# Filler matmuls of identity by ones at the opening and at both layer norms of a decoder layer

## The chip, the cores and the metric

The kernel runs on one core of a Trainium2 chip. A core has a matrix engine (TensorE, PE in the profile), VectorE (DVE), ScalarE (ACT), GpSimd (POOL) and a queue engine that starts transfers (SyncE, SP). TensorE's clock is granted at one of two levels, 1.2 or 2.4 GHz; the profile gives the granted clock of a stretch as a share of the full one. The metric is the device time of one execution in microseconds (us), the median of several runs.

## The reference

One layer of a hybrid decoder is computed for 512 prompt tokens with 16 learned tokens ahead of them, and for 8 single sample tokens. All arithmetic is float32. Cut to what matters here:

```python
x = layer_norm(jnp.concatenate([meta, x_prompt], axis=1), ln_in_g, ln_in_b)
q, k, v, qi, wi, ki, hq, kf, hi, log_f, hg = project(x, w_in[l], lb_all[l])   # x @ w_in, split
# indexer scores -> top-k keys -> attention over them (attn_o)
# gated linear recurrence in chunks of 128 (hg_o), per-head norm and gate
mix = merge_heads(attn_o, hg_o, hg, hg_norm_g[l], w_out[l])                   # ... @ w_out
x = layer_norm(ALPHA * x + mix, ln1_g[l], ln1_b[l])
x = layer_norm(ALPHA * x + swiglu(x, w_gate[l], w_up[l], w_down[l]), ln2_g[l], ln2_b[l])

def layer_norm(x, g, b):
    mu = jnp.mean(xf, -1, keepdims=True)
    var = jnp.mean(jnp.square(xf - mu), -1, keepdims=True)
    return (xf - mu) * lax.rsqrt(var + LN_EPS) * g + b
```

The width is 2048, the inner width of the SwiGLU 5632. The samples take the same path, with keys and values from a paged cache. Outputs are the new x of both kinds of tokens, and the keys, values, indexer keys and states.

## The kernel before, in words

The kernel is written engine by engine: each engine has one block with its instructions in the order in which they run, and semaphores are the only thing that ties them together. So the order of TensorE is that of the text of its block, `def _(pe)`.

The activations lie turned, with the feature index on the 128 partitions and the 536 tokens (16 learned, 8 samples, 512 prompt) in the free dimension; 16 blocks k of 128 features make the width (`KD` = 16). Products run in three passes: ScalarE rounds an operand to a high part, VectorE subtracts it from the operand for the low part, and TensorE adds high by high, high by low and low by high (`wh`, `wl` for weights, `xh`, `xl` for x). The semaphore `h_split` counts ScalarE's parts, `l_split` VectorE's. Weights arrive by transfers that SyncE issues.

Opening. x arrives by tokens and is normalised in place (`xtok`). TensorE turns it block by block: `x_turn(k)` (L1419 and on) makes five transposes, four of 128 tokens and one of the 24 others. ScalarE or VectorE then applies gain and bias (`x_lin0`, `x_lin1`), ScalarE makes `xh`, VectorE `xl` (semaphore `xl_ready`). TensorE does `x_turn(0)`, `x_turn(1)`, and then `two_products`, which waits for the splits of the first two weight tiles (VectorE L1887) and goes through k: in each step `x_step(k)` turns block k + 2 and waits for `xl` of block k, and twelve products of 260 columns follow (L1405).

First layer norm. When the last of the 16 output blocks of the mixer is added (VectorE L2346, semaphore `s_done`), VectorE adds it to a running sum (`finish`, L2321, semaphore `s_sum`) and, after ScalarE has squared it (L1192), to a running sum of squares (L2327, semaphore `q_sum`). Each counts 16 for a layer norm. `ln_sums(1)` on TensorE waits for both at 16 and multiplies a matrix of ones by the sums, which adds over the partitions (L1776 to L1779, results in the PSUM banks b4 to b7). VectorE forms means and variances (L2359 to L2364), ScalarE the reciprocal root, and then each block k is centred (L2372), scaled (L2380), given gain and bias (ScalarE L1253) and split (ScalarE L1256, VectorE L2398). TensorE waits for the split of block 0 and runs `first_pair`: twelve products for the gate weights with each block k, and in every second step twelve more for the up weights (helper `passes`, L1787).

SwiGLU. Gate and up products go by a scheme with seven products of half blocks for eight, whose sums of tokens and weights VectorE forms; hidden values go to memory and come back for the down product, 64 units of 11 blocks each.

Second layer norm. The same, with `ln_sums(2)`. Then TensorE turns the outputs back, in four quarters of 20 transposes (L1367): each quarter waits for four more blocks from ScalarE (L1349, semaphore `y_ready`). ScalarE and VectorE take turns in copying the turned banks out (L1355, L2592), and SyncE writes them.

`mm` is the plain matmul (output, stationary operand, moving operand), `ident` a 128x128 identity and `ones` a 128x128 matrix of ones, both float32. `acc` is four PSUM banks, indexed [:, tile parity, half, column].

Of the kernel before, what the change touches and what calls it, by code (L numbers as in the profile page):

```python
# [14 lines left out]
P = 128  # L15
# [167 lines left out]
def program(  # L183
# [6 lines left out]
    def sem(name):  # L190
        if name not in sems:
            sems[name] = ctx.enter_context(nc.semaphore(name))
        return sems[name]
# [41 lines left out]
    ident = rt.take("ident", [P, P])  # L235
    ones = rt.take("ones", [P, P])
# [163 lines left out]
    acc = ctx.enter_context(nc.psum_tensor("acc", [P, 2, 2, 512], F32))  # L400
# [3 lines left out]
    b7 = ctx.enter_context(nc.psum_tensor("b7", [P, 512], F32))  # L404
# [46 lines left out]
    def y_copied(u):  # L451

        return "y_act" if y_on_act(u) else "y_dve", len([v for v in range(u + 1) if y_on_act(v) == y_on_act(u)])

    def y_bank(u):
        u %= 8
        return (b4, b5, b6, b7)[u][:, :] if u < 4 else acc[:, (u - 4) // 2, u % 2, :]
# [902 lines left out]
    def _(pe):  # L1360
        mm = nc.tensor.matmul

        def turn(out, in_):

            k = in_.shape[0]
            b = in_.start_partition()
            return nc.tensor.transpose(out, in_, ident[b:b + k, b:b + k])  # L1367
# [21 lines left out]

        X = (xh, xl)  # L1390

        def two_products(s, t, before):

            pe.wait_ge(sem("l_split"), (s + 2).v)
            if t.const >= 2:
                for i in range(2):
                    pe.wait_ge(sem(f"acc_read{(t + i).odd}"), (t + i).half().v)
            for k in range(KD):
                before(k)
                for i in range(2):  # L1400
                    s_, t_ = s + i, t + i
                    a_h, a_l = (w[:, s_.odd, k * P:k * P + P] for w in (wh, wl))
                    for n, (a, b) in enumerate(((a_h, X[0]), (a_h, X[1]), (a_l, X[0]))):
                        for half in range(2):
                            ins = mm(acc[:, t_.odd, half, 0:LIVE], a, b[:, k, S0 + half * LIVE:S0 + half * LIVE + LIVE],  # L1405
                                     start=(k == 0 and n == 0), stop=(k == KD - 1 and n == 2))
                    if k == KD - 1:
                        ins.then_inc(sem("mm"), 1)
# [11 lines left out]
        def x_turn(k):  # L1420
            if k == 0:
                pe.wait_ge(sem("x_norm"), NB + 3)
            if k == 1:
                pe.wait_ge(sem("krow_ready"), 1)
            if k >= 2:
                pe.wait_ge(sem(f"x_lin{k % 2}"), k // 2)
            for c in range(NB):
                turn(real[k % 2][:, c * P:c * P + P], xtok[:, c, k * P:k * P + P])
            turn(small[k % 2][:, 0:R0], xtok_s[:, k * P:k * P + P]).then_inc(sem("x_turned"), 1)

        x_turn(0)
        x_turn(1)

        def x_step(k):
            if k + 2 < KD:
                x_turn(k + 2)
            pe.wait_ge(sem("xl_ready"), k + 1)

        def kx_turn(b):
# [5 lines left out]
            last.then_inc(sem("kx_turned"), 1)  # L1445

        two_products(At(0), At(0), x_step)
        for i in (2, 3):
            product(At(i), At(i), KD, P, 0, X, {5 * q + 3: (lambda b=3 * i - 6 + q: kx_turn(b),) for q in range(3)})
# [211 lines left out]
        for g in range(NG):  # L1661
            for j in range(4):
# [7 lines left out]
                else:  # L1670
                    n = 4 * (g - 1) + j
# [96 lines left out]

        def ln_sums(n):

            pe.wait_ge(sem("s_sum"), 16 * n)
            pe.wait_ge(sem("q_sum"), 16 * n)
            if n == 1:
                pe.wait_ge(sem("so_out"), NS)
            ssum = SUMS[n - 1]
            mm(b4[:, :], ones[:], ssum[:, 0, R0:NT], start=True, stop=True)  # L1776
            mm(b5[:, 0:NS], ones[:], ssum[:, 0, S0:R0], start=True, stop=True)
            mm(b6[:, :], ones[:], ssum[:, 1, R0:NT], start=True, stop=True)
            mm(b7[:, 0:NS], ones[:], ssum[:, 1, S0:R0], start=True, stop=True).then_inc(sem("ln_sums"), 1)  # L1779

        ln_sums(1)


        def passes(out, hi_, lo_, x_, xl_, first, last):
# [57 lines left out]
        for u in range(NU):  # L1842
# [8 lines left out]
            for k in range(CK):  # L1851
# [3 lines left out]
                for h in range(2):  # L1855
                    x_, xl_ = (b[c % 2][:, k, h * LIVE:h * LIVE + LIVE] for b in (hh, hl))
                    ins = passes(acc[:, u % 2, h, 0:LIVE], a_h, a_l, x_, xl_, k == 0, k == CK - 1)
            ins.then_inc(sem("mm"), 1)
        ln_sums(2)

        for q in range(4):
            pe.wait_ge(sem("y_ready"), 4 * q + 4)
# [2 lines left out]
            for c in range(NB + 1):  # L1865
                u = 5 * q + c
                if u >= 8:
                    name, n = y_copied(u - 8)
                    pe.wait_ge(sem(name), n)
                for k in range(4):  # L1870
                    out = y_bank(u)[:, P * k:P * k + P]
# [752 lines left out]
```

## Time and profile before

| | |
|---|---|
| median of three runs | 2597.6 us (2593.74 to 2597.88) |
| profiled execution, its own time | 2595.63 us |
| its span, first to last instruction | 2594.1 us |
| TensorE busy | 2513.6 us, 97% |
| VectorE busy | 1579.8 us, 61% |
| ScalarE busy | 967.1 us, 37% |
| mean granted TensorE clock | 0.986 |

The profile is of one execution. Its times count from the first instruction. Matmuls are pipelined, so a matmul's own duration is longer than the distance between the starts of two that follow each other; that distance is what a further one costs. A float32 matmul of full precision leaves two records, one of the three-pass kind leaves one. Some matmul records can be missing. The view of busy times by stretches has for each engine the busy time and in brackets the number of instructions; after POOL stand the granted TensorE clock, the share of the transfer engines and GB/s.

### The profile page before, as it was taken

The numbers are of one execution on the slowest core, as the hardware profiler recorded it, in microseconds if no ns is written. First come the engines' busy times: TensorE is split into PE (matmuls) and PEld (weight loads), VectorE is DVE, ScalarE is ACT, GpSimd is POOL, SyncE is SP. The second block draws the span as 40 slices with busy tenths as digits, with TensorE's granted clock in tenths as the row PEclk, the third lists the DMA queues.
The fourth block names the chain that finished last, engine by engine and source line by source line (L and its number), as shares of the span: only waits on it lengthen the run. The fifth ranks groups of instructions, "written<-read, shape, count | busy, mean of one in ns | idle before, by whom it ended". The sixth has DMA issues, their size and how long they took to land.

```text
span 2594.1 us, 47371 instructions
## 1 busy us (share of the span) xinstructions
PE 2513.6 (97%) x20365; PEld 2452.7 (95%) x20365; DVE 1579.8 (61%) x2225; ACT 967.1 (37%) x1542; POOL 173.1 (7%) x196
## 2 busy tenths in 40 slices
PE   6999999999999999989999999999999999999995
PEld 5989999999999988989999999999999999999995
DVE  6157776776766632588777777777777533333345
ACT  5344434343333422254444444444444321222123
POOL 1111111111000112000000000000000000000003
PEclk9989999999999999989999999999999999999998
DMA  4413333333322433333333333343333643333221
GB/s 137 113 51 83 98 82 82 92 93 87 103 83 77 128 108 93 116 113 107 128 109 128 118 106 131 107 131 115 110 127 109 229 156 103 123 102 110 90 68 66
DMA packets 292172, 279.52 MB, mean 108 GB/s; under 512 B 8344, under 2 KB 266696, under 8 KB 291464
## 3 DMA queue, kind: packets, MB, share of 16 engines
q1 hardware_dynamic: 284656, 255.18, 31.4%
q0 software_dynamic: 7344, 21.80, 2.9%
q8 instruction: 138, 2.26, 0.4%
q14 instruction: 34, 0.28, 0.0%
HBM read 247.54 MB, written 29.42 MB: 107 GB/s over the span
## 4 chain that ended last, share of the span: by engine, by line
PE 93%; DVE 4%; ACT 2%; issue 1%; DMA 1%; SPq 0%; ACTq 0%; DVEq 0%
PE acc L1787 47%; PE acc L1383 30%; PE b L1787 5%; PE b L1367 2%; PE acc L1405 1%; PE b L1528 1%; PE b L1649 1%; PE b L1624 1%; PE b L1544 1%; PE b L1705 1%; PE b L1725 1%; PE b L1556 1%; DVE lnd L2393 1%; PE b L1650 0%; PE b L1506 0%
## 5 line engine op out<-in xcount | busy, mean ns | idle before, releaser
L1383 PE MATMUL acc<-xh,wh 128*128 128x260 f32 (+2 forms) x2144 | 455.8, 294 | 6.1 <-DVE wl L1887 3.7
L1383 PE MATMUL acc<-xl,wh 128*128 128x260 f32 (+2 forms) x2144 | 439.0, 286 | 0.0
L1383 PE MATMUL acc<-xh,wl 128*128 128x260 f32 (+2 forms) x2144 | 438.9, 286 | 0.0
L1242 ACT ACTIVATE ph<-pair 128x1024 fp32r<-128x1024 f32 x252 | 267.3, 1061 | 413.6 <-PE acc L1787 405.2
L2404 DVE TENSOR_TENSOR pl<-pair,ph 128x1024 fp32r<-128x1024 f32 x252 | 308.5, 1224 | 158.9 <-ACT ph L1242 158.9
L1787 PE MATMUL acc<-hh,dh 128*128 128x260 f32 x1408 | 398.3, 283 | 3.6 <-DVE hl L2538 3.6
L1787 PE MATMUL acc<-hl,dh 128*128 128x260 f32 x1408 | 398.0, 283 | 0.0
L1787 PE MATMUL acc<-hh,dl 128*128 128x260 f32 x1408 | 397.8, 283 | 0.0
L1383 PEld LDWEIGHTS acc<-xh,wh 128*128 128x128 f32 (+1 forms) x2144 | 334.9, 191 | 15.2 <-DVE wl L1887 3.9
L1383 PEld LDWEIGHTS acc<-xh,wl 128*128 128x128 f32 (+1 forms) x2144 | 336.0, 191 | 0.0
L1383 PEld LDWEIGHTS acc<-xl,wh 128*128 128x128 f32 (+1 forms) x2144 | 335.8, 191 | 0.0
L1787 PE MATMUL acc<-xh,ph 128*128 128x260 f32 x1008 | 285.9, 284 | 1.4 <-DVE pl L2404 1.4
L1787 PE MATMUL acc<-xl,ph 128*128 128x260 f32 x1008 | 285.6, 283 | 0.0
L1787 PE MATMUL acc<-xt,pl 128*128 128x260 f32 x1008 | 285.3, 283 | 0.0
L1787 PE MATMUL acc<-xh,pl 128*128 128x260 f32 x1008 | 285.1, 283 | 0.0
L1787 PE MATMUL acc<-xtl,ph 128*128 128x260 f32 x1008 | 285.0, 283 | 0.0
L1787 PE MATMUL acc<-xt,ph 128*128 128x260 f32 x1008 | 284.0, 282 | 1.1 <-ACT part L1288 0.6
L1887 DVE TENSOR_TENSOR wl<-raw,wh 128x2048 fp32r<-128x2048 f32 (+1 forms) x69 | 159.0, 2306 | 184.7 <-ACT wh L817 166.7
L1787 PEld LDWEIGHTS acc<-hh,dh 128*128 128x128 f32 x1408 | 265.5, 189 | 4.6 <-DVE hl L2538 4.6
L1787 PEld LDWEIGHTS acc<-hl,dh 128*128 128x128 f32 x1408 | 265.2, 188 | 0.0
L1787 PEld LDWEIGHTS acc<-hh,dl 128*128 128x128 f32 x1408 | 265.1, 188 | 0.0
L817 ACT ACTIVATE wh<-raw 128x2048 fp32r<-128x2048 f32 x68 | 129.6, 1907 | 172.4 <-PE acc L1383 169.8
(436 smaller groups left out, 4441.1 us busy)
## 6 DMA issues: line engine op xcount, KB each, us to landing
raw<-in_w_in_dram SPq DMA_DIRECT2D x52, 1024.0 KB, 5.6
draw<-in_w_down_dram SPq DMA_DIRECT2D x32, 1408.0 KB, 6.6
pair<-in_w_gate_dram SPq DMA_DIRECT2D x42, 1024.0 KB, 5.3
pair<-in_w_up_dram SPq DMA_DIRECT2D x42, 1024.0 KB, 5.0
raw<-in_w_out_dram SPq DMA_DIRECT2D x16, 1024.0 KB, 5.6
hid_dram<-hid SPq DMA_DIRECT2D x22, 520.0 KB, 3.2
stg<-hid_dram SPq DMA_DIRECT2D x44, 260.0 KB, 6.7
sacc<-x_dram SPq DMA_DIRECT2D x6, 1040.0 KB, 7.7
```

The source lines that it names most:

```text
L817: act.activation(wh[:, s.odd, :], raw[:, s.odd, :], ACT.Copy).then_inc(sem("h_split"), 1)
L1242: act.activation(ph[n % 3][:, :, :], block_of(q, i), ACT.Copy).then_inc(sem("h_split"), 1)
L1367: return nc.tensor.transpose(out, in_, ident[b:b + k, b:b + k])
L1383: ins = mm(acc[0:rows, t.odd, half, 0:n_], a, b[:, kx0 + k, lo + half * n_:lo + half * n_ + n_], start=(k == 0 and n == 0), stop=(k == kt ...
L1405: ins = mm(acc[:, t_.odd, half, 0:LIVE], a, b[:, k, S0 + half * LIVE:S0 + half * LIVE + LIVE], start=(k == 0 and n == 0), stop=(k == KD - ...
L1528: last = mm(b7[0:w, P * c + SUB * i:P * c + SUB * i + SUB], et[:, off + c * w:off + c * w + w], qd[:, R0 + P * c + SUB * i:R0 + P * c + SU ...
L1544: last = mm((b6, b7)[b // 4][:, P * (b % 4):P * (b % 4) + P], ident[0:NS, b:b + 1].to_broadcast([NS, P]), itok[0:NS, 5, :], start=True, st ...
L1556: last = mm(b5[:, S0 + b:S0 + b + 1], ss[:, b, :], hq[:, S0 + b:S0 + b + 1], start=True, stop=True)
L1624: mm((b4, b5)[hd][:, 0:w], q[:, hd, lo:lo + P], k[:, R0:R0 + w], start=True, stop=True)
L1787: ins = mm(out, a, b, start=first and n == 0, stop=last and n == 2, skip_group_check=True)
L1887: V.tensor_tensor(wl[:, s.odd, 0:n], raw[:, s.odd, 0:n], fr(wh[:, s.odd, 0:n]), ALU.subtract)\
L2404: V.tensor_tensor(pl[n % 3][:, :, :], block_of(q, i), fr(ph[n % 3][:, :, :]), ALU.subtract).then_inc(sem("l_split"), 1)
```

## The change

A helper `keep_awake(out, count)` on TensorE multiplies the identity by the ones `count` times, into 128 columns of a bank that is free at that time. Nobody reads the result and no semaphore is raised. It is called at five places:

- opening: 20 after `x_turn(1)`, ahead of `two_products`
- in `ln_sums`, thus at both layer norms: 10, ahead of the wait for the last sums, behind a new wait for the last but one of them
- after `ln_sums(1)`: 32; after `ln_sums(2)`: 56

```diff
+        def keep_awake(out, count):
+
+            for _ in range(count):
+                mm(out, ident[:], ones[:], start=True, stop=True)
+
...
         x_turn(0)
         x_turn(1)
+        keep_awake(acc[:, 1, 1, 0:P], 20)
 
...
         def ln_sums(n):
 
+            pe.wait_ge(sem("s_sum"), 16 * n - 1)
+            keep_awake(b7[:, 0:P], 10)
             pe.wait_ge(sem("s_sum"), 16 * n)
             pe.wait_ge(sem("q_sum"), 16 * n)
...
         ln_sums(1)
+        keep_awake(acc[:, 0, 1, 0:P], 32)
 
...
         ln_sums(2)
+        keep_awake(acc[:, 0, 1, 0:P], 56)
```

TensorE at the opening, before. A row is a line, an operation, output<-inputs (moving operand first), the size and how many in a row:

```order
L1367 MATMUL b<-ident,vrows 128x113
L1417 MATMUL b<-ptT,pageof 128x8
L1367 MATMUL b<-ident,xtok 128x128 x4
L1367 MATMUL b<-ident,xtok_s 128x24
L1367 MATMUL b<-ident,xtok 128x128 x4
L1367 MATMUL b<-ident,xtok_s 128x24
L1367 MATMUL b<-ident,xtok 128x128 x4
```

The same place in the changed kernel:

```order
L1367 MATMUL b<-ident,xtok 128x128 x4
L1367 MATMUL b<-ident,xtok_s 128x24
L1395 MATMUL acc<-ones,ident 128x128 x20
L1367 MATMUL b<-ident,xtok 128x128 x4
L1367 MATMUL b<-ident,xtok_s 128x24
L1410 MATMUL acc<-xh,wh 128x260 x2
L1410 MATMUL acc<-xl,wh 128x260 x2
```

Twenty matmuls stand between the turns of block 1 and of block 2; nothing else has moved, only the line numbers.

TensorE at the first layer norm, before (the last products of the mixer, the sums, the first pair):

```order
L1383 MATMUL acc<-xh,wl 128x260 x2
L1776 MATMUL b<-ssum_146,ones 128x512
L1777 MATMUL b<-ssum_146,ones 128x8
L1778 MATMUL b<-ssum_146,ones 128x512
L1779 MATMUL b<-ssum_146,ones 128x8
L1787 MATMUL acc<-xh,fh_153 128x260
```

And in the changed kernel:

```order
L1383 MATMUL acc<-xh,wl 128x260 x2
L1395 MATMUL b<-ones,ident 128x128 x10
L1784 MATMUL b<-ssum_146,ones 128x512
L1785 MATMUL b<-ssum_146,ones 128x8
L1786 MATMUL b<-ssum_146,ones 128x512
L1787 MATMUL b<-ssum_146,ones 128x8
L1395 MATMUL acc<-ones,ident 128x128 x32
L1796 MATMUL acc<-xh,fh_153 128x260
```

Ten stand ahead of the sums and 32 behind them.

TensorE at the second layer norm in the changed kernel (before, the two rows of L1395 are missing):

```order
L1796 MATMUL acc<-hh_186,dl_184 128x260
L1395 MATMUL b<-ones,ident 128x128 x10
L1784 MATMUL b<-ssum_193,ones 128x512
L1785 MATMUL b<-ssum_193,ones 128x8
L1786 MATMUL b<-ssum_193,ones 128x512
L1787 MATMUL b<-ssum_193,ones 128x8
L1395 MATMUL acc<-ones,ident 128x128 x56
L1367 MATMUL b<-ident,sacc 128x128 x16
```

Ten stand ahead of the sums and 56 between them and the turns of the first quarter.

## Rows read from the trace of the kernel before

**Rows 1.** The page: busy time; clock in 40 slices; chain by engine.
```profile
PE 2513.6 (97%) x20365; PEld 2452.7 (95%) x20365; DVE 1579.8 (61%) x2225; ACT 967.1 (37%) x1542; POOL 173.1 (7%) x196
...
PEclk9989999999999999989999999999999999999998
...
PE 93%; DVE 4%; ACT 2%; issue 1%; DMA 1%; SPq 0%; ACTq 0%; DVEq 0%
```

**Rows 2.** Order in time, TensorE, opening: start, us, line, operation, [idle before <-releaser].
```profile
22.46 1.12 PE L1367 MATMUL b<-ident,xtok 128*128 128x128 f32 x4
...
29.32 1.11 PE L1367 MATMUL b<-ident,xtok 128*128 128x128 f32 x4 [4.25 <-DVE wl L1887]
...
33.36 0.96 PE L1367 MATMUL b<-ident,xtok 128*128 128x128 f32 x4
...
35.97 0.60 PE L1367 MATMUL b<-ident,xtok 128*128 128x128 f32 x4
...
38.19 0.60 PE L1367 MATMUL b<-ident,xtok 128*128 128x128 f32 x4
```

**Rows 3.** Order in time, VectorE, opening.
```profile
24.78 4.48 DVE L1887 TENSOR_TENSOR wl<-raw,wh 128x2048 fp32r<-128x2048 f32 x2
29.18 1.34 DVE L1936 TENSOR_TENSOR xl<-lnt,xh 128x536 fp32r<-128x536 f32 x2
...
32.44 0.72 DVE L1936 TENSOR_TENSOR xl<-lnt,xh 128x536 fp32r<-128x536 f32 x1 [0.72 <-ACT xh L864]
```

**Rows 4.** Order in time, TensorE, first layer norm.
```profile
1131.85 1.10 PE L1776 MATMUL b<-ssum,ones 128*128 128x512 f32 x2 [2.36 <-DVE ssum L2321]
...
1134.52 0.44 PE L1779 MATMUL b<-ssum,ones 128*128 128x8 f32 x2
1141.83 0.56 PE L1787 MATMUL acc<-xh,fh 128*128 128x260 f32 x1 [6.87 <-DVE xl L2398]
```

**Rows 5.** Busy time by stretches: stretch, length, engines, clock, transfers.
```profile
1132.90:1135.00 2.10, 2.06 (x7) 0.97 (x5) 2.10 (x2) 0.00 (x0) 0.00 (x0) 0.57 0.00 0
...
1141.80:1146.70 4.90, 4.87 (x22) 4.90 (x23) 4.90 (x9) 3.56 (x6) 0.00 (x0) 0.50 0.17 56
...
2559.50:2569.00 9.50, 0.00 (x0) 0.00 (x0) 8.32 (x7) 4.24 (x7) 8.13 (x6) 0.52 0.00 0
2569.00:2573.30 4.30, 4.20 (x20) 3.79 (x20) 4.27 (x4) 3.26 (x6) 3.46 (x3) 0.50 0.01 4
2573.30:2576.00 2.70, 1.94 (x17) 1.61 (x16) 2.70 (x6) 1.97 (x3) 1.35 (x1) 0.94 0.07 27
```

**Rows 6.** Order in time, all engines, second layer norm.
```profile
2554.57 1.10 PE L1776 MATMUL b<-ssum,ones 128*128 128x512 f32 x2 [2.40 <-DVE ssum L2327]
...
2556.59 0.28 PE L1779 MATMUL b<-ssum,ones 128*128 128x8 f32 x2
...
2568.23 2.96 ACT L1349 ACTIVATE sacc<-lnd,vec 128x520 f32<-128x520 f32 x4 [2.57 <-DVE lnd L2393]
...
2569.10 3.68 PE L1367 MATMUL b<-ident,sacc 128*128 128x128 f32 x16 [12.23 <-ACT sacc L1349]
```

**Rows 7.** Order in time, TensorE, a head's output, all between at 128 columns.
```profile
224.09 0.38 PE L1552 MATMUL b<-aT,itok 128*128 128x128 f32 x2
...
225.87 1.28 PE L1556 MATMUL b<-hq,ss 128*128 128x1 f32 x11
```

**Rows 8.** Order in time, VectorE, first layer norm.
```profile
1132.73 2.29 DVE L2333 TENSOR_TENSOR fl<-first,fh 128x2048 fp32r<-128x2048 f32 x1 [0.98 <-ACT fh L1200]
...
1135.00 0.76 DVE L2359 TENSOR_SCALAR mu<-b 128x512 f32<-128x512 f32 x2
...
1140.98 0.70 DVE L2398 TENSOR_TENSOR xl<-sacc,xh 128x520 fp32r<-128x520 f32 x1 [0.34 <-ACT xh L1256]
...
1142.82 0.69 DVE L2398 TENSOR_TENSOR xl<-sacc,xh 128x520 fp32r<-128x520 f32 x1
```

**Rows 9.** The chain that ended last, in order of time, one piece of SwiGLU.
```profile
1216.01 17.30 PE acc L1787 x144
```

## The prediction

> **What bounds the kernel now.** I read the page's busy line, its clock line and the shares of the chain first [rows 1]. The reader is to see three things: TensorE is busy for 97% of the span, the chain that ends last is 93% TensorE, and the clock granted to TensorE is full nearly everywhere. So the kernel is a stream of matmuls, and only two kinds of time are left to an edit of this sort: places where TensorE stands still, and places where it works at the lower of its two clocks, 1.2 instead of 2.4 GHz. An added matmul in a pause doesn't shorten the pause. It can only raise the clock for what follows. So I went to the three pauses that the edit fills, with the order in time of TensorE and VectorE there, and then to the table by stretches for the granted clock.
>
> Opening: the ten transposes of x, begun at 22.46, end at 25.07, TensorE then stands until 29.32, where VectorE's two splits of the first weights end (24.78 + 4.48), and goes on with steps of one turn and twelve products [rows 2, 3]. The first of these steps takes 33.36 - 29.32 = 4.04 us, the second 2.61, the third 2.22, and so do the following ones. Same instructions, 1.82 times the time: TensorE is at 1.2 GHz until about 34. (The page's clock line shows a 9 for the first slice; it begins with the first recorded change, so here I go by the durations.) First layer norm: pause of 2.36 us before the sums, then, after them, 6.87 us until the first split of x1 is there [rows 4]. The clock falls during the sums (0.57), and is at 0.50 for the first 4.9 us of work after the pause [rows 5]. Second layer norm: 2.40 us before the sums, 12.23 after them, and clock 0.50 in the 4.3 us in which the first turns run [rows 5, 6].
>
> **The price of one added matmul.** It is a 128x128 float32 matrix times 128 float32 columns, two records each. The nearest rows are the eight of that shape and type in a head's output: 224.09 to 225.87 us, so 1.78 / 8 = 0.222 us at full clock [rows 7]. At 1.2 GHz I take twice that, 0.44 (the opening's steps say 1.82 times, 0.40). The added wait (one short of the last sum) never binds: that sum is done while TensorE still multiplies, and nobody waits for the new matmuls, which signal nothing. What they can cost is only to run past the end of the pause.
>
> **Opening, 20 matmuls.** At full clock they take 4.44 us and would end at 29.52; each microsecond of the block that is spent at 1.2 GHz adds half a microsecond. So all hangs on when the clock rises. Rises in the trace came 4.4 to 4.8 us after work resumed at 29.32 (the surplus of the two slow steps is 1.82 + 0.39 = 2.21 us, twice that is 4.4), 4.9 after 1141.83, and some 4.3 after 2569.10 [rows 2, 4 to 6]. In the changed kernel work without a pause begins with the transposes at 22.46, so I expect the rise near 22.46 + 4.6 = 27.1. That is 2.0 us into the block, which then ends at 29.52 + 1.0 = 30.5, or 1.2 us later than TensorE could have gone on. Against that stand the 2.21 us of surplus, since the steps now run at 2.22 from the first. Do the others keep up? The second split of x is ready at 29.18 + 1.34 = 30.52, before the second step at 32.7; the third ends at 32.44 + 0.72 = 33.16 today and is wanted at about 35.5 [rows 3]. Yes. Sum: **-1.0 us**. Bounds: -2.0 if the clock is up from the block's first matmul, +0.3 if it rises only 4.9 us after 25.07 (then the end is 32.0, 2.7 late, against 2.2 to 2.4), +4.6 if it never rises.
>
> Here a rule of the Trainium skill speaks against the change. The row: in the last layer norm nothing but transposes runs from 2569.10, and the clock goes from 0.50 to 0.94 in the stretch after 2573.30 [rows 5, 6]. The page "TensorE: Matmul & The Clock Gate", Part 4 on the PE-mode transpose, says that the full clock isn't engaged by transposes, as they don't count as busy in the same way. By that rule the opening would come out at +0.3, by the row at -1.0; the trace disagrees with the page, and I go by the row.
>
> **First layer norm, 10 and 32 matmuls.** The ten take 2.2 us of the 2.36 that TensorE waits anyway: nothing. They keep the clock up through the sums, whose four products then take 2556.59 - 2554.57 = 2.02 us from first to last instead of 2.67 [rows 4, 6]. But that buys nothing: VectorE works at its own split of a weight until 1135.02 and takes the means at 1135.00 as it is [rows 8]. From there the next thing to come is the same, at 1141.83. The 32 start at about 1134.0 and take 7.1 us, to 1141.1: 0.7 us to spare. Then the first pairs start warm: 4.9 us at 1.2 GHz become 4.9 / 1.82 = 2.7, which saves 2.2. What is late next is x1's second split, ready at 1142.82 + 0.69 = 1143.51 [rows 8], when twelve products of 17.30 / 144 = 0.12 us [rows 9] end at 1143.27: 0.3 us given back. After that a pair of steps costs TensorE 36 x 0.12 = 4.3 us and VectorE 3.7 (its splits start 1.84 us apart, at 1140.98 and 1142.82), so it isn't caught again. The next waits on the way, VectorE's sums of token blocks and the loads of weights, start when TensorE has finished, so they move with it. Sum: **-1.9 us**. Bounds: -2.5 (a before with a longer slow stretch), -1.2 (0.26 us a matmul, so that the 32 run over by 0.7).
>
> **Second layer norm, 10 and 56 matmuls.** The ten are hidden as before. The 56 take 12.4 us from 2556.7, to 2569.1, which is where the fourth output is ready (the first of ScalarE's four pieces from 2568.23) and the turns start at 2569.10 today [rows 6]. The twenty turns then run at full clock, 2.2 us instead of 4.3. But what follows is paced by VectorE, busy for 4.27 of 4.30 us there [rows 5], and its chain of centring and scaling doesn't wait for these turns. So **0 us**, from -0.5 (a copy that ScalarE does earlier) to +1.9: the last twenty turns lie on the path, TensorE pauses three more times before them, and if their rise of the clock comes later than today they take twice as long.
>
> Together -1.0 - 1.9 + 0 = **-2.9 us**. The profiled execution took 2595.63, so it would take 2592.7. The median of the runs shown is 2597.6, 2.0 above it; I set the change against the median: **2594.7 us**, or 0.11% less.
>
> **Rivals.** *The transposes don't count.* Then the opening gives +0.3 to +0.5 and the total is -1.5: 2596.1. For it: in the opening the transposes at 22.46 are followed by a pause, so that place shows nothing; against it the last layer norm.
>
> *The clock's own moments.* The clock falls and rises at moments that the program doesn't set, so a slow stretch in the pauses that stay (before the turns of the last quarters, or between the selection's products) may drop out or be shortened too. With the best bounds, -2.0 - 2.5 - 0.5 = -5.0, and a little from those: 2592.3.
>
> *Slower: identity by ones doesn't hold the clock.* Its operands are constants, mostly zeros, and no row shows a matmul of two constants. If it counts for nothing the clock falls at 1132.9 and 2559.5 as today, and the blocks overrun at 0.44 us each. Opening: 20 x 0.44 = 8.8, end at 33.9, +4.6. First norm: 32 x 0.44 = 14.1 from 1134.7 to 1148.8, +7.0. Second: 12 at full clock, 44 x 0.44 = 19.4, to 2578.9, 9.8 late, of which some 8 reach the end. Total +20: 2617. The point from which it decides is whether the granted clock in the 32 is 1.0: above 0.22 us a matmul the 32 have 0.7 us of room, so from about 0.245 on they cost.
>
> **How the numbers follow.** A measurement here tells about 0.2% (5.2 us) from no change. Forecast, -2.9: 0.66. Transposes don't count: 0.14. More than the sum, about -5: 0.13. Identity by ones doesn't hold the clock: 0.07. Faster by over 0.2% needs more than 5.2 us, which takes the third case and half of it is still short, with a little from the first's tail and from the scatter of the medians: 0.12. Slower is the last case: 0.07. Within 0.2%: 0.81. The runs shown lie 4 us apart, so I add 1.5 us to the cases' ends: from 2592.3 - 1.5 = 2590.8 to 2596.1 + 1.9 (last turns slow) + 0.6 = 2598.6.
>
> **What would show it right or wrong.** Right: in the opening the added line runs from 25.1 to about 30.5, its first five or so matmuls at 0.44 and the rest at 0.222 us, and the third step starts near 35.0 instead of 35.97. In the first norm the granted clock stays at 1.0, the means are still taken behind VectorE's split, the first pair starts no later than before, counted from the end of the product ahead of it, and its 24 first products take 0.12 us each with one short wait. In the second the first turns start within 0.2 us of today's time and the end moves only as far as the start did. Wrong: a granted clock of 0.50 inside the added blocks, a block that ends behind what it waits for, VectorE waiting for turns at the end, or a gain at the first norm that later waits of VectorE take back.

## The result, and the profile after

The changed kernel takes 2590.77 us, median of 20 runs (2586.13 to 2596.93), against 2596.30 of the kernel before in the same measurement (20 runs, 2593.14 to 2599.84): ratio 0.9977, interval 0.9970 to 0.9983. That is 5.5 us less (by the interval 4.4 to 7.8), and 0.03 us below the foot of the stated range. The forecast was 2.9 us less, which lies outside the interval. The direction was right, the size half of what came. Of the 3.9 us between the forecast time of 2594.7 and 2590.77, 1.3 are the start: the forecast counted from the median of three executions, 2597.6, and twenty give 2596.30. A ratio with its interval compares executions taken side by side, so it isn't quite the quotient of the two medians. Two executions of later measurements lie far outside the others (4116 us at a granted clock of 0.56, and 13,894 us) and are left out of every median.

The page of the changed kernel, the lines that answer to [rows 1]: TensorE's busy time, its clock in 40 slices, the chain by engine.

```profile
PE 2535.9 (98%) x20621; PEld 2475.5 (96%) x20621; DVE 1580.1 (61%) x2225; ACT 966.8 (37%) x1542; POOL 173.3 (7%) x196
...
PEclk9999999999999999999999999999999999999999
...
PE 93%; DVE 3%; ACT 2%; issue 1%; DMA 1%; SPq 0%; ACTq 0%; DVEq 0%
```

TensorE is busy 22 us longer, with 256 more records (two for each of the 128 added matmuls), and the kernel is shorter. The three 8s in the clock line of before (a slice is a fortieth of the span) are gone. The profiled execution took 2590.7 us (span 2589.2), 4.9 less than that of before.

The opening in order of time, TensorE (start, us, line, operation), against [rows 2]:

```profile
22.87 1.11 PE L1367 MATMUL b<-ident,xtok 128*128 128x128 f32 x4
...
24.15 5.96 PE L1395 MATMUL acc<-ones,ident 128*128 128x128 f32 x40
29.95 0.60 PE L1367 MATMUL b<-ident,xtok 128*128 128x128 f32 x4
...
32.19 0.60 PE L1367 MATMUL b<-ident,xtok 128*128 128x128 f32 x4
...
34.43 0.60 PE L1367 MATMUL b<-ident,xtok 128*128 128x128 f32 x4
```

The block starts right behind the turns and lasts 29.95 - 24.15 = 5.80 us where 20 x 0.222 = 4.44 were counted at full clock: 1.36 more, so 2.7 us of it were at the lower clock (the record of the granted clock has the rise at 26.76, 2.6 us into the block). From there the steps take 2.24 us from the first. This execution's loads were in 0.9 us sooner, so all times stand that much earlier; measured from the transposes' end (24.15 and 25.07), the third step starts 10.28 us behind it and 10.90 before.

The first layer norm, TensorE, against [rows 4]; the figure in brackets is the pause and what ended it:

```profile
1125.42 2.39 PE L1395 MATMUL b<-ones,ident 128*128 128x128 f32 x20
1127.94 1.10 PE L1784 MATMUL b<-ssum,ones 128*128 128x512 f32 x2
...
1129.95 0.28 PE L1787 MATMUL b<-ssum,ones 128*128 128x8 f32 x2
1130.09 7.39 PE L1395 MATMUL acc<-ones,ident 128*128 128x128 f32 x64
1137.86 0.36 PE L1796 MATMUL acc<-xh,fh 128*128 128x260 f32 x1 [0.38 <-DVE xl L2408]
```

And its granted clock by stretches (TensorE busy, weight loads, VectorE, ScalarE, GpSimd, clock, transfers), against [rows 5]:

```profile
1128.00:1130.00 2.00, 2.00 (x8) 1.04 (x8) 1.19 (x1) 0.78 (x1) 0.00 (x0) 1.00 0.00 0
1130.00:1137.50 7.50, 7.48 (x67) 7.29 (x65) 6.87 (x12) 3.25 (x5) 0.00 (x0) 1.00 0.72 239
1137.80:1141.00 3.20, 3.08 (x23) 2.90 (x24) 3.20 (x6) 2.23 (x4) 0.00 (x0) 1.00 0.20 66
```

The clock stays at 1.0 through the sums, the block and the first pairs. The block of 32 ends 0.38 us before the first split of x1 is there. VectorE, against [rows 8], still works at its split of a weight when the sums are done at 1130.1, and takes the means behind it:

```profile
1128.81 2.29 DVE L2343 TENSOR_TENSOR fl<-first,fh 128x2048 fp32r<-128x2048 f32 x1 [0.98 <-ACT fh L1200]
1131.02 0.76 DVE L2369 TENSOR_SCALAR mu<-b 128x512 f32<-128x512 f32 x2
```

The second layer norm, TensorE, against [rows 6]:

```profile
2546.99 2.39 PE L1395 MATMUL b<-ones,ident 128*128 128x128 f32 x20
2549.56 1.10 PE L1784 MATMUL b<-ssum,ones 128*128 128x512 f32 x2 [0.17 <-DVE ssum L2337]
...
2551.71 12.75 PE L1395 MATMUL acc<-ones,ident 128*128 128x128 f32 x112
2564.30 1.91 PE L1367 MATMUL b<-ident,sacc 128*128 128x128 f32 x16
2566.05 0.60 PE L1367 MATMUL acc<-ident,sacc 128*8 128x128 f32 x4
2569.45 2.63 PE L1367 MATMUL acc<-ident,sacc 128*128 128x128 f32 x12 [2.80 <-ACT sacc L1349]
```

The first turns are done 2.35 us after their start instead of 4.3, and then TensorE waits 2.80 us for the next outputs: their speed is worth nothing.

So each block does in its place what was forecast. Between the two profiles the time went as follows, counted in ScalarE's instructions, which are the same in both: loads 0.9 (not the change's), opening to block 9 of x 0.7, from there to 200 us **2.4**, first layer norm to the first half-block sums 2.0, second layer norm 0.0, and 0.9 given back in the hand-over to the down product, at about 2040 to 2050, where hidden values come back from memory. The forecast had no term for the 2.4 us. These are two executions; how far they stand for the kernels, the table at the end shows.

### The profile page after: what moved, and what is told of

Its sections match the earlier page's. It is cut to its first block, busy times and chain, and to the rows that moved or that the text cites. A ratio compares the mean times of both kernels' runs of the same rounds, so it can differ in the third digit from the quotient of the medians.

```text
span 2589.2 us, 47883 instructions
## 1 busy us (share of the span) xinstructions
PE 2535.9 (98%) x20621; PEld 2475.5 (96%) x20621; DVE 1580.1 (61%) x2225; ACT 966.8 (37%) x1542; POOL 173.3 (7%) x196
## 4 chain that ended last, share of the span: by engine, by line
PE 93%; DVE 3%; ACT 2%; issue 1%; DMA 1%; SPq 0%; ACTq 0%; DVEq 0%
PE acc L1796 47%; PE acc L1383 30%; PE b L1796 5%; PE b L1367 2%; PE acc L1410 1%; PE b L1534 1%; PE b L1655 1%; PE b L1630 1%; PE b L1550 1%; PE b L1711 1%; DVE lnd L2403 1%; PE b L1731 1%; PE b L1562 1%; PE b L1656 0%; PE b L1512 0%
## 5 line engine op out<-in xcount | busy, mean ns | idle before, releaser
L817 ACT ACTIVATE wh<-raw 128x2048 fp32r<-128x2048 f32 x68 | 129.6, 1907 | 172.3 <-PE acc L1383 169.7
```

Source lines behind the costliest of these rows:

```text
L817: act.activation(wh[:, s.odd, :], raw[:, s.odd, :], ACT.Copy).then_inc(sem("h_split"), 1)
```

## The experiments

In the diffs `keep_awake(out, n)` is the change's helper; kernels "of before" have only the lines shown. Times are medians; "before" is the kernel before in the same measurement. Each measurement of a kernel also gives one profile, and from these I take the five stages of the table at the end.

**Each part alone.** Opening only:

```diff
         x_turn(1)
+        keep_awake(acc[:, 1, 1, 0:P], 20)
```

> Only the 20 matmuls of the opening. The whole change gained 5.5 us by the medians, forecast 2.9. Theory A (parts as forecast, the rest chance): -1.0 us against before, inside the noise, and the added block ends 1 to 1.5 us after VectorE's second split. Theory B (the opening moves all later work against the clock's own moments, and slow stretches between 60 and 200 us get shorter because of it): -3 to -3.5 us, and in the profile the stretches at clock 0.50 near 68 and 140 us are shorter than before's 6.8 us. Theory C (the unforeseen gain sits at the end): -1.0.

Measured 2596.18 against 2595.93, ratio 0.9999 (0.9991 to 1.0008).

First layer norm only:

```diff
         def ln_sums(n):
+            if n == 1:
+                pe.wait_ge(sem("s_sum"), 16 * n - 1)
+                keep_awake(b7[:, 0:P], 10)
...
         ln_sums(1)
+        keep_awake(acc[:, 0, 1, 0:P], 32)
```

> Only the first layer norm: 10 matmuls ahead of the sums and 32 behind them. Theories A, B and C: -1.9 us, from 4.9 us of half clock that go and 0.3 us of a new wait for the second split of x1. A rival, D: before's slow stretch after the pause is on the average longer than in its profile, then -2.5 to -3.

Measured 2595.85, ratio 1.0003 (0.9994 to 1.0012).

Second layer norm only (the same with `n == 2`, and 56 behind `ln_sums(2)`):

> Only the second layer norm: 10 matmuls ahead of the sums and 56 behind them. Theories A and B: 0 us, since VectorE's chain paces the end. Theory C (the end of before mostly has its last quarter of turns, or those before it, at half clock, and the filler changes that): -1.5 to -2.5 us, and in the profile the last turn starts nearer to the sums than before's 31.6 us (2586.2 - 2554.6).

Measured 2594.37, ratio 0.9994 (0.9985 to 1.0002).

The parts add up to 1.4 us, not to 5.5, and each interval is 4.4 us wide. As measurements of time they say little: executions of one kernel scatter by 2 to 3 us (standard deviation). Their profiles say more. That of the first norm has no slow stretch there, and its root to half-block sums is 1.9 us shorter, as forecast. That of the second shows nothing at the norm against the profile of before. But the two in which the second norm isn't filled differ from before's: from the square of the last block to the root 7.74 and 7.75 us, where before has 6.30. The profile of before was a quick one in this place.

**Do transposes keep the clock up?** As the first norm only, with

```diff
-                mm(out, ident[:], ones[:], start=True, stop=True)
+                nc.tensor.transpose(out, ones[:], ident[:])
...
-                keep_awake(b7[:, 0:P], 10)
+                keep_awake(b7[:, 0:P], 20)
...
-        keep_awake(acc[:, 0, 1, 0:P], 32)
+        keep_awake(acc[:, 0, 1, 0:P], 62)
```

> As the kernel with only the first layer norm filled, but the filler is a transpose of the ones (20 ahead of the sums, 62 behind them) in place of identity by ones. If transposes count as work for the clock: the granted clock stays at 1.0 from the sums to the first pair, and the time is -1.9 us as with matmuls. If they don't: the clock falls within the sums or the block, the 62 take up to twice their 7 to 8 us, and the time is +5 us or more.

Measured 2594.17 against 2595.93, ratio 0.9995 (0.9985 to 1.0005). The profile by stretches, sums, block and first pairs:

```profile
1129.50:1131.80 2.30, 2.13 (x8) 1.21 (x9) 1.32 (x2) 1.01 (x1) 0.00 (x0) 1.00 0.00 0
1131.80:1139.00 7.20, 6.99 (x65) 6.75 (x63) 6.57 (x12) 3.02 (x5) 0.00 (x0) 1.00 0.73 237
1139.00:1142.00 3.00, 2.34 (x17) 2.17 (x18) 3.00 (x6) 2.33 (x4) 0.00 (x0) 1.00 0.44 136
```

Seven microseconds of nothing but transposes hold the clock at 1.0. The page "TensorE: Matmul & The Clock Gate" of the Trainium skill, Part 4, says that the full clock doesn't engage for transposes, which don't count as busy in the same way. This trace doesn't agree: 62 transposes in a row kept the granted clock at 1.00, and in [rows 5] transposes came before its rise from 0.50 to 0.94.

**The whole again, more pauses, the tens alone, and twice the block.** The whole change unaltered:

> The whole change once more. Alone, none of the three parts moved the median by more than 1.6 us (+0.2, -0.1, -1.6), while the whole moved it by 5.5. Theory A (the parts add up, the first measurement of the whole had luck with the moments at which the clock falls): -3 to -4 us against before. Theory B (the parts help one another): -5 to -6 again.

Measured 2589.44 against 2596.01, ratio 0.9964 (0.9950 to 0.9978): 6.6 us by the medians, 9.3 by the ratio. The first measurement wasn't luck.

The whole change and four more fillers, in the pauses between 60 and 1040 us; the added waits are those that the next product has anyway:

```diff
         two_products(At(0), At(0), x_step)
+        keep_awake(b6[:, 0:P], 15)
...
         def idx_scores(i, m):
...
+            if n in (0, 10):
+                pe.wait_ge(sem("acc_read1"), At({0: 7, 10: 9}[n]).half().v)
+                keep_awake(acc[:, 1, 1, 0:P], {0: 7, 10: 10}[n])
...
+        pe.wait_ge(sem(f"acc_read{At(T_D2).odd}"), At(T_D2).half().v)
+        keep_awake(acc[:, At(T_D2).odd, 1, 0:P], 8)
         att_in(0)()
```

> The whole change, and the same filler in the four further pauses of TensorE between 60 and 1040 us: 15 before the third weight tile (pause 3.7 us), 7 and 10 before two of the selection's products (1.8 and 2.5), 8 before the second half of the output projection (2.0). If the scatter of the stage from the opening to 200 us (149.8 to 153.1 us in six profiles) is the clock falling after such pauses: that stage takes 147 to 149 us, and the kernel 2 to 4 us less than the whole change. If the filler overruns the pauses, nothing or a loss of up to 2 us.

Measured 2586.48 against 2596.01, ratio 0.9956 (0.9942 to 0.9970). That is 9.5 us less than the kernel before, and 3.0 less than the whole change in the same measurement. The stretch from 60 to 200 us in the profile of before and of this kernel:

```profile
60.00:200.00 140.00, 130.68 (x1012) 122.25 (x1011) 50.68 (x73) 55.63 (x138) 19.24 (x19) 0.93 0.29 77
```

```profile
60.00:200.00 140.00, 136.69 (x1135) 129.04 (x1134) 54.13 (x81) 58.62 (x145) 19.23 (x19) 1.00 0.32 85
```

The granted clock is 0.93 before and 1.00 here; in the changed kernel it is 0.95. In these two profiles that is where the missing 2.4 us are: in this stretch before had three slow stretches of 6.8 us, and the changed kernel, which the diff doesn't touch there, has two of 3.4 and one of 6.8. Before, then the changed kernel:

```profile
68.20:75.00 6.80, 5.43 (x25) 5.43 (x26) 3.61 (x2) 1.78 (x2) 0.00 (x0) 0.50 0.68 166
139.90:146.70 6.80, 6.27 (x36) 5.66 (x35) 4.11 (x13) 2.63 (x14) 0.00 (x0) 0.50 0.22 58
177.50:184.30 6.80, 6.07 (x24) 4.73 (x26) 2.54 (x4) 1.70 (x8) 0.00 (x0) 0.50 0.30 76
```

```profile
67.70:71.10 3.40, 3.06 (x14) 3.06 (x15) 2.58 (x2) 0.74 (x2) 0.00 (x0) 0.50 0.66 158
71.20:78.00 6.80, 6.80 (x60) 6.80 (x59) 0.00 (x0) 1.20 (x2) 1.64 (x2) 1.00 0.73 199
136.00:139.40 3.40, 3.40 (x22) 3.13 (x19) 1.69 (x6) 2.61 (x7) 0.00 (x0) 0.50 0.90 243
139.50:143.00 3.50, 3.09 (x32) 2.83 (x31) 2.29 (x9) 1.20 (x8) 0.00 (x0) 1.00 0.00 0
173.50:180.30 6.80, 6.01 (x24) 4.74 (x26) 2.54 (x4) 1.76 (x8) 0.00 (x0) 0.50 0.30 78
```

The tens alone (only the two lines in `ln_sums`):

> Only the ten matmuls ahead of the sums at both layer norms. In two of four profiles without them the second norm took 7.75 us from the last addition to the means instead of 6.30, because the clock fell before or in the sums; at the first norm 13.4 instead of 12.7 in one. Theory A: with the ten both are 6.30 and 12.7 in every profile, worth 0.5 to 1 us on the average, which the forecast had at nothing. The forecast as it stood: 0.

Measured 2596.22 against 2596.01, ratio 0.9997 (0.9988 to 1.0006): not to be told from nothing. In its profile the sums take what they take at full clock, 6.30 us to the root at the second norm, and the clock falls in the pause behind them.

Twice the block at the first norm (64 for 32, otherwise the whole change):

> The whole change with 64 instead of 32 matmuls behind the first sums. At 0.222 us each they end at 14.2 us behind the sums, where the first split is ready after 7.7: TensorE is 6.5 us late. By then all 16 splits are ahead, so the wait of 0.2 us for the second goes: +6.3 us against the whole change. If overrun is partly hidden by VectorE later: less.

Measured 2597.72; against the whole change of this measurement, 2589.44, that is 8.3 us more. In the profile the block lasts 14.2 us and from the root to the half-block sums it takes 6.2 us more than in the changed kernel (43.22 and 37.03 in the table's measure), as expected. The other 2 us are no more than the uncertainty of the two means. An overrun here is paid in full.

**Does the opening shift what follows?** Ten matmuls that only delay, behind the wait for the first weights, nothing else:

```diff
         x_turn(1)
+        pe.wait_ge(sem("l_split"), 2)
+        keep_awake(acc[:, 1, 1, 0:P], 10)
```

> Kernel before with ten of the filler matmuls behind the wait for the first two splits of weights, where they can only delay: they move all that follows by 2.2 us against the moment at which the clock rises in the opening. In nine profiles the stretch from VectorE's split of block 7 of x to 200 us takes 149.6 to 150.1 us where the rise came 19.0 to 20.2 us ahead of that split, and 152.2 to 153.1 where it came 13.6 to 14.5 ahead; with the opening filled it was always the former. Theory B (the opening's filler sets where the later pauses fall against the clock's moments): the rise is now about 2 us earlier against the work, the stretch takes 149.6 to 150.5 in the profile, and of the 2.2 us of delay some 1.6 come back: 0 to +1.5 us. Theory A (chance, or the filler itself): the stretch stays at 152 in most executions, +2.2 us.

Measured 2599.07 against 2596.61, ratio 1.0016 (1.0003 to 1.0029): 2.5 us more by the medians, 4.2 by the ratio. The ten, in order of time:

```profile
28.49 3.85 PE L1395 MATMUL acc<-ones,ident 128*128 128x128 f32 x20 [4.25 <-DVE wl L1894]
```

They took 3.7 us, not the 2.2 counted at full clock, because the clock rose only at 31.36, 2.9 us into them. The opening's own stage took 25.2 us against 23.8 on the average of the kernels without its filler, so some 2.3 us of the delay came back in the first steps, which then ran at full clock. In the stretch to 200 us nothing came back: 152.2 us, which is what theory A expected.

The expectation also counted badly: of the nine profiles two without the opening's filler had the short stretch too (149.8), with the rise 12.8 and 12.9 us ahead, and it names only the others. And the late ten put the rise 17.3 us ahead, between its two groups, where no other profile without fillers in the later pauses lies. So theory B's forecast failed, but the test didn't reach the distance that B speaks of, and what it tells against B is little.

Opening and first norm (the whole change without the second):

> The whole change without the second layer norm. By the stages of the profiles so far: opening -0.7, the stretch to 200 us -1.6, first norm -1.8, and the second norm's sums at half clock in about half of the executions as before: -4 us. If the parts only help one another as a whole: -2 or less.

Measured 2591.40 against 2596.61, ratio 0.9978 (0.9969 to 0.9987): 5.2 us, where 4 were expected.

Both norms without the opening:

> The whole change without the opening. Theory B: first norm -1.8, second -0.7, and the scatter of the stretch to 200 us stays that of before: -2.5 us, 3 to 4 us less gain than the whole. Theory A: within 1 us of the whole change, -5.

Measured 2593.74, ratio 0.9993 (0.9984 to 1.0003): 2.9 us, 2.6 to 3.7 less than the whole gained. So within the whole the opening is worth about 3 us, give or take as much again: the interval alone is 4.9 us wide.

Four more fillers, with 14 instead of 20 in the opening:

> The kernel with fillers in the four further pauses, with 14 instead of 20 matmuls in the opening. Twenty end 1.5 us after VectorE's splits are ready; 14 are 6 x 0.222 = 1.3 us shorter, and the clock is up before they end in most executions: -0.5 to -1.3 us against the same kernel with 20, 2585.5 to 2586. If the clock is still low when they end, the first step is slow and it is +0.5.

Measured 2587.46, ratio 0.9964 (0.9952 to 0.9976); with 20 it was 2586.48. The expected 0.5 to 1.3 us didn't come. In the profile the opening's stage is 22.1 us, 1.4 less than with 20, but a slow stretch of 3.4 us follows at 133.6. The profiled execution, at 2593.02 the slowest of six, lost its time elsewhere: from 200 to 1120 us it took 929.1 us, against 924.9 and 926.5 in the two profiles with 20. With six and five executions the two counts can't be told apart.

**Is it the pauses?** The four further fillers alone:

> Kernel before with fillers only in the four further pauses (15, 7, 10 and 8 matmuls). If the clock's falls after the pauses are the scatter of the stretch to 200 us: it takes 145.6 to 147.1 us as in the two profiles with these fillers, whatever the opening does, against 149.7 to 153.1, and the kernel is 4 to 5 us below the kernel before (some of it lost again where a fall comes later in the heads). If the scatter is something else in the opening: 149 us and more, and -2 us or less.

Measured 2592.80 against 2596.59, ratio 0.9983 (0.9973 to 0.9993): 3.8 us. The stretch takes 147.1 us, as in the kernel with 14 in the opening, and less than in any of the profiles without these fillers (148.4 to 153.1). So what makes it long, and most of its scatter, is the clock's fall at these pauses.

Opening only, again:

> Only the opening's 20 matmuls, a second time (first: +0.2 us by the medians, -0.9 by the means). Theory B (0.7 in its own stage and 1.6 on the way to 200 us): -2.3 us, the stretch to 200 us below 150.5 in the profile. Theory A (chance): -0.7 us, and the stretch may be 152 or more.

Measured 2592.65 against 2596.59, ratio 0.9988 (0.9980 to 0.9997): 3.9 us by the medians, 3.1 by the ratio; the stretch 148.4 us.

The kernel before, again:

> The kernel before, unchanged, for one more profile of it and the size of chance: within 1.5 us of the kernel before. The opening's stage 23.2 to 24.5 us, the stretch to 200 us anywhere from 149.6 to 153.1.

Measured 2596.16 against 2596.59, ratio 0.9998 (0.9989 to 1.0007). The stretch takes 152.1 us. And its second norm isn't the one of [rows 6]: TensorE's sums, with the granted clock in them.

```profile
2555.12 1.65 PE L1775 MATMUL b<-ssum,ones 128*128 128x512 f32 x2 [2.40 <-DVE ssum L2326]
2556.56 0.43 PE L1776 MATMUL b<-ssum,ones 128*128 128x8 f32 x2
2556.85 2.05 PE L1777 MATMUL b<-ssum,ones 128*128 128x512 f32 x2
2558.70 0.41 PE L1778 MATMUL b<-ssum,ones 128*128 128x8 f32 x2
```

```profile
2555.50:2558.90 3.40, 3.40 (x8) 1.64 (x6) 0.00 (x0) 0.00 (x0) 0.00 (x0) 0.50 0.00 0
```

The same kernel, the same pause of 2.40 us, and here the clock had fallen when the sums ran: 2558.70 - 2555.12 = 3.58 us from the first to the last instead of 2.02.

All fillers, again:

> The whole change and the four further pauses, a second time (first: 2586.5 us, five runs). If it beats the changed kernel: 2586 to 2588, 8 to 10 us below the kernel before. If the first was luck: 2590.

Measured 2586.48 against 2596.59, ratio 0.9958 (0.9945 to 0.9971). Twice 2586.48: that is some 10 us below the kernel before, and 3.0 and 4.3 below the two medians of the changed kernel, 2589.44 and 2590.77.

**The stages over all profiles.** Each is measured between the starts of two instructions of ScalarE, in us: A, second weight split (L817) to gain and bias of block 9 of x (L859; it starts when VectorE has split block 7); B, from there to the first head's copy (L1006); C, square of the last but one block (L1192) to the first root (L1224) of the first norm; D, from 3.5 us behind that root, at x1's second block (L1253), to the second rounding of half-block sums (L1249); E, square of the last block to the root of the second norm. One profile is one execution.

| stage | not filled there | filled there | gain of the means | forecast |
|---|---|---|---|---|
| A, the opening's own | 23.2 to 24.4, mean 23.84 (8) | 22.8 to 24.1, mean 23.31 (8) | 0.5 | 1.0 |
| B, to 200 us, by whether the opening is filled | 149.7 to 153.1, mean 151.29 (7) | 148.4 to 150.1, mean 149.60 (6) | 1.7 | none |
| B, with fillers in its own pauses | | 145.6, 145.6, 147.1, 147.1 | 4.9 | none |
| C, first norm's sums | 12.72 to 13.56, mean 12.98 (7) | 12.71 to 12.72 | 0.3 | 0 |
| D, first pairs | 38.35 to 39.43, mean 38.98 (8) | 37.01 to 37.04 | 1.9 | 1.9 |
| E, second norm's sums | 6.30 (twice), 6.31, 7.28 to 7.99, mean 7.29 (9) | 6.30 to 6.31 | 1.0 | 0 |

The kernel with the late ten is left out of A and B, the one with 14 out of A and the doubled block out of D. The gains of A, B, C, D and E are 0.5 + 1.7 + 0.3 + 1.9 + 1.0 = 5.4 us, near the measured 5.5 and 6.6. That it agrees to 0.1 us is luck: the scatter makes the sum of the means uncertain by more than half a microsecond, the 0.3 of C comes wholly from the two profiles of the opening alone (13.43 and 13.56; the other five are at 12.72 to 12.80), and two long stages stand between these. From 200 us to C the profiles take 921.7 to 929.1 us, from D to E 1372.8 to 1375.2, with no difference between filled and unfilled that stands out of this scatter.

**Opening and stretch together.** Added up for each profile, A and B take 172.4 to 173.6 us with the opening filled (six) and 173.9 to 176.3 without (seven). The two groups don't overlap, and their means are 2.3 us apart.

**Where the clock rises against the work.** The time from the clock's rise in the opening to block 9 of x sorts B in all fourteen profiles without fillers in B's own pauses:

| from the rise to block 9, us | profiles | opening filled | B |
|---|---|---|---|
| 12.8 to 13.0 | 3 | no | 149.7 to 149.8 |
| 13.6 to 14.5 | 4 | no | 152.1 to 153.1 |
| 17.3 | 1 | late ten | 152.2 |
| 18.5 to 19.9 | 6 | yes | 148.4 to 150.1 |

## Why the prediction was half right

**What bounds the kernel: right.** The chain is 93% TensorE in both, the added matmuls shorten no pause, and all that was gained is work at the higher clock.

**The price of a matmul: right.** 32 of them from 1130.09 to 1137.48, 0.23 us each with the last one's tail in it (0.222 forecast). Identity by ones holds the clock, and raises it: in the kernel with the late ten TensorE had stood for 4.25 us, did nothing but these, and the clock rose 2.9 us into them. The rival in which it doesn't is dead.

**The opening's own stage: right in kind, half the size.** I had the rise 4.6 us after work began at 22.46. It came 2.6 us into the block, 5.2 after the turns' start at 21.60 (forecast 2.0 into the block), and the block ended 1.5 us after TensorE could have gone on, not 1.2. What failed is the fixed delay of the rise, taken from one execution. In the eight profiles with 20 in the opening the rise came 4.8 to 7.4 us after the turns' start and the block ended 1.4 to 2.6 us late, 1.9 on the average. So the stage gains 0.5, not 1.0.

**First norm: right.** The first ten fit in the pause, the means stay behind VectorE's own split, the 32 end 0.38 us early (0.7 forecast), 1.9 us come from the first pairs and one short wait for the second split stays. What I had at nothing, the sums, is worth 0.3 on the average: VectorE's split hides a slow set of sums only up to 0.7 us.

**Second norm: the turns right, the sums wrong.** "The ten are hidden as before ... So 0 us" held for the turns and for the execution that I had read. The step that failed is to take its 2.02 us for the sums as what the kernel does. In six of nine profiles without the ten the clock had fallen before the sums were through, and there nothing hides it: 1 to 1.7 us on the path, 1.0 on the average. The first norm's own row, where the clock does fall in the sums after a pause of the same length (0.57 in [rows 5]), should have told me that it can here.

**The term that was missing.** This is the step that failed first: the forecast counted the opening up to its third step and took all later work as moved by a constant, so the stretch to 200 us stood in the sum at nothing. It gains 1.7 us there on the average. I named the clock's own moments as a rival and priced it as chance, 0.13. The stretch up to 200 us has pauses of 1.8 to 3.7 us, the clock falls after them or not, and each fall costs TensorE work at half speed. That these pauses are the cause is shown: filled, the stretch takes 145.6 to 147.1 us with the opening filled or not. That filling the opening shortens it too is shown for A and B together, where the profiles with and without don't overlap (2.3 us, against 1.0 forecast); for B alone it is likely, since three of seven profiles without the filler are as short as those with it. The medians say the same loosely: the opening alone gained -0.2 and 3.9 us, and both norms with it gained 2.6 to 3.7 more than without it. How it does so is in part open. B follows the time between the clock's rise and the work. Without the filler that time lies on both sides of the step between 13.0 and 13.6 us, with it always at 18.5 to 19.9. That speaks for my account, that the filler fixes how the later pauses lie against the moments of the clock. No experiment set this time on purpose and got the short stretch: the one that tried, the late ten, landed at 17.3 us and had the long one.

**The start and the ends of the range.** The sum was set against 2597.6; against the 2596.30 of twenty executions the same sum gives 2593.4. The text says that 1.5 us were added at both ends of the range; at the upper end it added 0.6, which doesn't touch the lower end, where the time came out.

**Are the parts worth their sum?** Alone they measured 1.4 us together by the medians, where the whole gave 5.5 and 6.6. This doesn't show that they help one another: each part's interval is 4.4 us wide, and the opening alone gave 3.9 us the second time, which makes the sum 5.5. One effect between places is likely: with the opening alone both profiles had the first norm's sums slow (13.43 and 13.56 in stage C), and no other had. So a time moved at one place can meet a worse moment at the next. The ten ahead of the sums take that away at the two norms. Elsewhere the clock goes on falling: with all nine fillers both profiles still have six slow stretches of 3.4 us between 200 and 1000 us, and one such kernel scattered by 0.6 us in one measurement and by 2.5 in the other.

## What to carry to other kernels

Where TensorE bounds the kernel and waits for a few microseconds at a time, cheap matmuls in the pauses can pay twice: by the full clock right behind them, and by taking the slow executions out of a stage (6.30 us in every profile instead of 6.30 to 7.99). Size a block to end before its wait does: behind the first norm an overrun was paid in full. The opening's block overran by 1.4 to 2.6 us and still gained, because it stood in for steps that would have run at the lower clock. And before costing such an edit, read more than one execution, or bound each stage by both clocks: a pause after which the clock didn't fall in the profile at hand is no proof that it doesn't, and a rise of the clock comes at another time in the next execution.

## What the runs showed of the hardware

The clock also falls while TensorE has no pause. In the changed kernel, in a head: sixteen records of a matmul with 8 of 128 rows (L1550), and soon behind it a slow stretch, TensorE busy for all of both.

```profile
327.31 2.05 PE L1550 MATMUL b<-itok,ident 8*128 8x128 f32 x16
329.28 0.51 PE L1383 MATMUL acc<-xh,wh 128*128 128x260 f32 x2
```

```profile
327.00:330.50 3.50, 3.50 (x29) 3.23 (x29) 1.14 (x1) 2.42 (x2) 0.00 (x0) 1.00 0.00 0
330.60:333.90 3.30, 3.30 (x18) 3.30 (x17) 2.90 (x8) 0.00 (x0) 0.00 (x0) 0.50 0.27 70
```

So the clock fell behind 3.5 us in which TensorE was busy throughout; what in them let it fall, this case doesn't separate. The same sixteen records stand ahead of the first fall behind 200 us with all nine fillers too (206.53, fall at 209.5). There is no pause there that a filler could take. It also falls while a short pause is still going on: before the output projection's second half TensorE stood for 2.0 us, 1033.1 to 1035.1 in the kernel before, and the clock fell at 1034.2. Beyond that, 7.0 us of nothing but 128x128 transposes held the clock at 1.0, and so did 7.4 us of matmuls of two constants.
